# Moving the first pair of every feed-forward block to other PSUM banks, and three reorderings around it

## The reference

```python
for l in range(2):
    x = x + 0.5 * swiglu(rmsnorm(x, ffn1_norm[l]), ffn1_wg[l], ffn1_wu[l], ffn1_wd[l])   # FFN 0, FFN 2
    h = rmsnorm(x, mix_norm[l]) @ w_in[l]
    ...                                   # three attention mixers (latent, sparse, differential)
    x = x + o @ w_out[l]
    x = x + 0.5 * swiglu(rmsnorm(x, ffn2_norm[l]), ffn2_wg[l], ffn2_wu[l], ffn2_wd[l])   # FFN 1, FFN 3
x = rmsnorm(x, final_norm)
...            # a second block: dilated attention, a gated recurrence, 16 experts with chosen tokens
# swiglu(x, wg, wu, wd) = (silu(x @ wg) * (x @ wu)) @ wd, with 2816 hidden units
# rmsnorm(x, g) = x / sqrt(mean(x * x) + 1e-6) * g
```

## Time and profile before

| | value |
|---|---|
| median of 3 runs | 3041.17 us |
| lowest, highest | 3035.72, 3044.26 us |
| the profiled execution | 3043.22 us, its span 3041.4 us |
| mean granted TensorE clock | 0.978 |
| PE, DVE, ACT, POOL busy | 94%, 67%, 38%, 55% of the span |

### The profile page before, as it was taken

How to read it: one execution, slowest core, us unless ns; L and a number is a source line. 1 busy time by engine, 2 the same in 40 slices (tenths; PEclk the granted TensorE clock), 3 DMA queues, 4 the chain that set the end, 5 groups by cost and what they waited for, 6 DMA issues and landing times.

```text
span 3041.4 us, 47934 instructions
## 1 busy us (share of the span) xinstructions
PE 2859.9 (94%) x19208; PEld 2309.7 (76%) x19208; DVE 2038.9 (67%) x2752; ACT 1145.4 (38%) x2098; POOL 1682.9 (55%) x969
## 2 busy tenths in 40 slices
PE   7999999999999999999999999999998687999888
PEld 6999867668999979998666788998796675555444
DVE  8888675758888889897767589897546764112112
ACT  5333332545333353434235443434245841111111
POOL 6999744446988779784644488785443640000000
PEclk9999999999999999999999999999999888999999
DMA  4322312002232322323300032323230015999997
GB/s 154 116 93 91 132 63 105 2 2 106 96 118 91 118 84 91 117 86 118 123 23 2 29 125 85 119 89 136 83 125 1 22 42 222 407 423 423 423 423 318
DMA packets 51769, 412.44 MB, mean 136 GB/s; under 512 B 5728, under 2 KB 5984, under 8 KB 24416
## 3 DMA queue, kind: packets, MB, share of 16 engines
q1 hardware_dynamic: 51408, 408.03, 34.4%
q0 software_dynamic: 144, 1.38, 0.1%
HBM read 407.29 MB, written 2.10 MB: 135 GB/s over the span
## 4 chain that ended last, share of the span: by engine, by line
PE 71%; DVE 12%; DMA 6%; issue 5%; ACT 3%; POOL 3%; SPq 0%; DVEq 0%; ACTq 0%; POOLq 0%
PE banks L1916 7%; PE banks L1917 7%; PE banks L1918 7%; PE banks L2213 6%; PE banks L1845 6%; PE banks L1714 5%; PE banks L1933 5%; PE banks L1934 5%; PE banks L1935 5%; DMA experts<-moe_w 4%; PE banks L1793 3%; PE banks L2224 3%; PE banks L1983 2%; DMA ring<-ffn_w 2%; PE banks L2011 2%
## 5 line engine op out<-in xcount | busy, mean ns | idle before, releaser
L930 POOL TENSOR_TENSOR ring_lo<-ring,w_hi 128x1024 fp32r<-128x1024 f32 x252 | 700.3, 2792 | 154.9 <-ACT w_hi L1087 98.3
L1087 ACT ACTIVATE w_hi<-ring 128x1024 fp32r<-128x1024 f32 x256 | 270.7, 1058 | 439.9 <-PE banks L1918 430.9
L1933 PE MATMUL banks<-ffn_hidden,down_hi 128*128 128x512 f32 x704 | 276.7, 393 | 9.5 <-DVE x L2596 9.5
L1934 PE MATMUL banks<-ffn_hidden,down_hi 128*128 128x512 f32 x704 | 276.1, 392 | 0.0
L1935 PE MATMUL banks<-ffn_hidden,down_lo 128*128 128x512 f32 x704 | 275.9, 392 | 0.0
L1916 PE MATMUL banks<-t_lo,w_hi 128*128 128x256 f32 x960 | 271.9, 283 | 1.3 <-POOL ring_lo L930 1.3
L2596 DVE SCALAR_TENSOR_TENSOR x<-banks,x 128x512 f32<-128x512 f32 x352 | 230.2, 683 | 60.2 <-PE banks L1935 58.6
L1917 PE MATMUL banks<-t_hi,w_hi 128*128 128x256 f32 x960 | 269.5, 281 | 0.0
L1918 PE MATMUL banks<-t_hi,ring_lo 128*128 128x256 f32 x800 | 225.4, 282 | 0.0
L2213 PE MATMUL banks<-experts,mix 128*64 128x256 f32 x1520 | 190.4, 392 | 17.1 <-DMA experts<-moe_w 17.0
L1916 PE MATMUL banks<-upper_lo,w_hi 128*128 128x256 f32 x640 | 183.6, 287 | 19.6 <-ACT ffn_more L1170 8.7
(11 more groups left out here) (448 smaller groups left out, 8227.1 us busy)
## 6 DMA issues: line engine op xcount, KB each, us to landing
experts<-moe_w SPq DMA_DIRECT2D x47, 2048.0 KB, 18.9
ring<-ffn_w SPq DMA_DIRECT2D x43, 2048.0 KB, 7.6
experts<-moe_w SPq DMA_DIRECT2D x48, 1024.0 KB, 18.7
ring<-mix_w SPq DMA_DIRECT2D x24, 1536.0 KB, 6.4
ring<-second_w SPq DMA_DIRECT2D x16, 1536.0 KB, 6.2
ffn_more<-ffn_w SPq DMA_DIRECT2D x44, 512.0 KB, 3.8
mix<-ffn_w SPq DMA_DIRECT2D x44, 512.0 KB, 7.9
expert_table<-moe_w SPq DMA_DIRECT2D x16, 1024.0 KB, 15.6
```

The costliest lines, as they stand in the source:

```text
L930: pool.tensor_tensor(operand_lo(G, i), operand(G, i), operand_hi(G, i).bitcast(F32), ALU.subtract).then_inc(w_split, 1)
L1087: act.activation(operand_hi(G, i), operand(G, i), ACT.Copy).then_inc(w_high, 1)
L1933: mm(bank[4 + q % 4], w_hi, g[:, f, 1], start=f == 0, stop=False)
L1934: mm(bank[4 + q % 4], w_hi, g[:, f, 0], start=False, stop=False)
```

## The change

It has three parts.

1. The four tiles of pair 0 go to banks 2 to 5 instead of 0 to 3, so product 0 of pair 1 no longer waits for DVE to read banks 0 and 1; the wait for pair 0's gate and hidden units moves to product 4. Product 1 of pair 0 waits for the adds that free banks 4 and 5. Around it, lists are reordered: on ACT `high(G+1, 1)`, `high(G+1, 2)` and the two corners of product 0 come earlier; on DVE `sums(G+1, 2)` comes before the mean in FFN 0 and 2, and before the gate in FFN 1 and 3; on POOL `low(G+1, 1)` of FFN 0 comes before T3 and T2.
2. The groups of the rotation tables on POOL stand at the end of pairs 1 to 9 instead of 2 to 10, and the three `rope_reduce` of a table stand together.
3. The low parts `h_lo` of x for the mixer are made between the last adds of FFN 0 and FFN 2 instead of after them.

```diff
 POOL, pair 0
                     low(G + 1, 0)
+                    if F == 0:
+                        low(G + 1, 1)
                     t3_difference(F)
                     t2_difference(F)
-                    low(G + 1, 1, 2)
+                    if F:
+                        low(G + 1, 1)
+                    low(G + 1, 2)
                     down_low(G, 0)
 POOL, end of a pair
+                if F == 0 and j in (1, 4, 7):
+                    rope_angle(j // 3)
                 if F == 0 and j in (2, 5, 8):
-                    rope_angle(j // 3)
-                    rope_reduce(j // 3, 0)
+                    for part in range(3):
+                        rope_reduce(j // 3, part)
                 if F == 0 and j in (3, 6, 9):
-                    rope_reduce(j // 3 - 1, 1)
-                    rope_reduce(j // 3 - 1, 2)
-                if F == 0 and j in (4, 7, 10):
                     rope_ends(j // 3 - 1)
 ACT, pair 0 and pairs 1 to 10
                     high_t1(F)
+                    high(G + 1, 1)
                     act.wait_ge(mean_ready, c.next(mean_ready))
                     act.activation(rms, rms, ACT.Sqrt).then_inc(root_ready, 1)
                     load_table(ACT.Silu)
+                    high(G + 1, 2)
                     high_t3(F)
                     silu(G, 0)
-                    high(G + 1, 1)
                     high_t2(F)
-                    high(G + 1, 2)
                     down_high(G, 0)
+                    corner(G + 1, 0, 0)
+                    corner(G + 1, 0, 1)
                     high_t4(F)
                     continue
                 high(G, 3)
-                corner(G, 0, 0)
-                corner(G, 0, 1)
+                if j > 1:
+                    corner(G, 0, 0)
+                    corner(G, 0, 1)
 PE, first_product and product
-                        if i < 2 and G:
-                            pe.wait_ge((gate_scaled, hidden_ready)[a], 2 * G - 1 + i)
-                        o = two_halves(bank[a + 2 * (i % 2)])
+                        if i == 0 and G:
+                            pe.wait_ge((gate_scaled, hidden_ready)[a], 2 * G)
+                        if i == 1 and G:
+                            pe.wait_ge(down_used, KC * G - 4 + a + 1)
+                        o = two_halves(bank[2 + a + 2 * (i % 2)])
 ...
-                        if i == 0:
+                        if i == 0 and j > 1:
                             pe.wait_ge((gate_scaled, hidden_ready)[a], 2 * G - 1)
                         if i == 4:
-                            pe.wait_ge((gate_scaled, hidden_ready)[a], 2 * G)
+                            pe.wait_ge((gate_scaled, hidden_ready)[a], 2 * G if j > 1 else 2 * G - 1)
 DVE, mixer_inputs
-            x_rest(COL_MIX + 8 * l, h_hi, h_lo, *range(KC))
             x_sum(*range(1, KC))
 DVE, pair 0 (its reads of banks 0 to 3 become reads of banks 2 to 5)
                     sums(G + 1, 0, 1)
+                    if F % 2 == 0:
+                        sums(G + 1, 2)
                     dve.wait_ge(sums_ready, c.next(sums_ready))
 ...
                     step(V.reciprocal(rms, rms))
+                    if F % 2:
+                        dve.wait_ge(t_pool, 4 * F + 2)
+                        sums(G + 1, 2)
                     first_gate(G)
                     first_scaled(G)
-                    if F % 2:
-                        dve.wait_ge(t_pool, 4 * F + 2)
-                    sums(G + 1, 2)
                     first_hidden(G)
 DVE, last pair
                     add(G, q)
                     if F == 1 and q:
                         x_lows(F + 1, q - 1)
+                    if F % 2 == 0 and q:
+                        x_rest(COL_MIX + 8 * (F // 2), h_hi, h_lo, q - 1)
                 if F == 1:
                     x_lows(F + 1, KC - 1)
+                if F % 2 == 0:
+                    x_rest(COL_MIX + 8 * (F // 2), h_hi, h_lo, KC - 1)
```

More of the change, by code:

```diff
@@ L2549, in first_gate @@
                 dve.wait_ge(strassen, 2 * turn(G, 2) + 1)
-            V.tensor_tensor(GATES[0], bank[0], rms, ALU.mult).then_inc(gate_scaled, 1)
+            V.tensor_tensor(GATES[0], bank[2 if opens(G) else 0], rms, ALU.mult).then_inc(gate_scaled, 1)
         def parts(G, f, product):
@@ L2559, in first_scaled @@
                 dve.wait_ge(strassen, 2 * turn(G, 2) + 2)
-            step(V.tensor_tensor(bank[1], bank[1], rms, ALU.mult))
+            up = bank[3 if opens(G) else 1]
+            step(V.tensor_tensor(up, up, rms, ALU.mult))
         def first_hidden(G):
             dve.wait_ge(silu_ready, 2 * G + 1)
-            step(V.tensor_tensor(bank[1], bank[1], GATES[0], ALU.mult))
+            up = bank[3 if opens(G) else 1]
+            step(V.tensor_tensor(up, up, GATES[0], ALU.mult))
         def second_gate(G):
@@ L2569, in second_gate @@
             if opens(G):
-                V.tensor_tensor(GATES[1], bank[2], rms, ALU.mult).then_inc(gate_scaled, 1)
+                V.tensor_tensor(GATES[1], bank[4], rms, ALU.mult).then_inc(gate_scaled, 1)
                 return
@@ L2579, in second_hidden @@
             dve.wait_ge(strassen, pair_done(G))
+            up = bank[5 if opens(G) else 3]
             if opens(G):
-                step(V.tensor_tensor(bank[3], bank[3], rms, ALU.mult))
+                step(V.tensor_tensor(up, up, rms, ALU.mult))
             else:
@@ L2587, in second_hidden @@
             dve.wait_ge(silu_ready, 2 * G + 2)
-            step(V.tensor_tensor(bank[3], bank[3], GATES[1], ALU.mult))
-            parts(G, 1, bank[3])
+            step(V.tensor_tensor(up, up, GATES[1], ALU.mult))
+            parts(G, 1, up)
         def add(G, *list_):
@@ L2598, in ffn @@
         def ffn(F):
+            c.skip(x_high, 12)
             for j in range(FFN_PAIRS):
@@ L2608, in ffn @@
                     step(V.reciprocal(rms, rms))
+                    if F % 2:
+                        dve.wait_ge(t_pool, 4 * F + 2)
+                        sums(G + 1, 2)
                     first_gate(G)
                     first_scaled(G)
-                    if F % 2:
-                        dve.wait_ge(t_pool, 4 * F + 2)
-                    sums(G + 1, 2)
                     first_hidden(G)
-                    parts(G, 0, bank[1])
+                    parts(G, 0, bank[3])
                     make_t4(F)
@@ L2661, in ffn @@
                         x_lows(F + 1, q - 1)
+                    if F % 2 == 0 and q:
+                        x_rest(COL_MIX + 8 * (F // 2), h_hi, h_lo, q - 1)
                 if F == 1:
                     x_lows(F + 1, KC - 1)
+                if F % 2 == 0:
+                    x_rest(COL_MIX + 8 * (F // 2), h_hi, h_lo, KC - 1)
             c.one(down_used, KC * FFN_PAIRS)
             c.skip(down_ready, KC * FFN_PAIRS)
-            c.skip(x_high, 12)
         def mixed(F):
```

## The result

The changed kernel takes 3047.16 us in the median of 10 runs (3040.87 to 3055.34), the kernel before 3040.97 (3033.89 to 3047.64) beside it. The ratio is 1.0031, with a 95% interval of 1.0018 to 1.0045: slower by 0.3%, 6 us by the medians and 9 by the ratio. The forecast was 3044, with a range from 3029 to 3053. The profiled execution took 3047.59 us, span 3045.8, 4.4 us longer than the span of before.

What follows compares the result with a forecast made beforehand. PE, busy 94% of the span, was taken as the bound, so only its waits could be won. Terms of -0.4 + 4 - 1.8 + 0.9 = +2.7 us on 3041.17 gave 3043.9 us, range 3029 to 3053.

Steps and rivals of the forecast that it cites:

- The second gate: FFN 0, first pairs: DVE reaches this gate at 51.2 instead of 51.47, so product 2 starts 0.3 us sooner.
- 4 us in one piece: FFN 2, pair 1: PE idles this long ahead of product 2; the term for FFN 2 was +0.5 us.
- Part 1, size: First pairs of the four feed-forward blocks: -0.3 in FFN 0, -0.6 in FFN 1 and 3, +0.5 in FFN 2, sum -0.4 us.
- the clock cost: FFN 0, first pairs: lower PE clock costs the same as before, give or take 0.5 us.
- Tables +4 in FFN 0: FFN 0, pairs 2 to 9: POOL's regrouped tables make PE wait, +4 us, bounds -2 and +8.
- -6.8 at the mixer: First mixer: with sooner tables and nothing else changed, PE's 4.14 us wait goes and the clock is kept, -6.8 us.
- pairs 2 to 9: FFN 0: PE's gains and losses pair by pair under the moved tables, less some 1.6 us for overlap, taken as +4.
- Part 3, first mixer: x_rest(0) holds up DVE's adds, taking most of the sooner tables' gain: -1.8 us, bounds -6.8 and +1.5.
- Part 3, second mixer: Last low part of x and sums of squares end 0.9 us later: +0.9 us, bounds -0.3 and +3.
- the sum of +2.7: Whole kernel: all terms, -0.4 + 4 - 1.8 + 0.9, added to the median of 3041.17 us, giving 3043.9.
- The case at 3051: Rival: POOL becomes the bound in FFN 0 (8 us) and the lock at the mixer falls badly, +10 us; chance 0.22.

Runs made afterwards that it cites:

- e2: Part 2 alone (tables regrouped and one pair sooner) on the kernel before: ratio 0.9990 (0.9981 to 0.9999), -3.0 us.
- e1: Part 1 alone on the kernel before, tables and low parts of x as before: ratio 1.0014 (1.0005 to 1.0024), +4.3 us.
- e3: Part 3 alone on the kernel before, tables late as before: ratio 1.0011 (1.0001 to 1.0021), +3.3 us.
- e4: The changed kernel with part 3 undone, parts 1 and 2 kept: ratio to the kernel before 1.0009 (0.9999 to 1.0019).
- e9: The kernel before with the last corner's sum written to its own bank instead of SBUF: ratio 1.0024 (1.0010 to 1.0037).
- e12: The kernel before with ungrouped-as-before tables one pair sooner, 2 MB load first, last corner's sum in its bank, part 1 with corners copied sooner: ratio 1.0007.
- e8: The kernel before with tables one pair sooner in their old groups and pair 3's 2 MB load ahead of the 0.5 MB one: 0.9983, 3034.32 us.

## Why the prediction came out as it did

- *Part 1, place and order.* The gaps moved and did not close. Product 0 had no wait, and PE idled 4.55 us in one piece ahead of product 2, for L1175. The second gate stood at 51.50 where I had 51.2. I hadn't said that product 1 would wait as well (6.86 us, since product 0's corners are now behind two high parts, a silu and a down piece); product 2 starts no later for it. In FFN 2 I had 4 us in one piece ahead of product 2, and it was 2.52 and 2.68 us in two.
- *Part 1, size.* In the two traces it gives +0.3 in FFN 0, -0.4, +0.2 and -0.4 in FFN 1 to 3, so -0.3 where I had -0.4. That this agrees is luck of two executions: timed alone part 1 is +4.3 (1.5 to 7.3). This is the term that was mis-sized. Over 12 traces the first pairs are 2.0 us longer with it, for +1.3 in FFN 0 (forecast -0.3) and +1.0 in FFN 2 (forecast +0.5). I had the clock cost "the same as before, give or take 0.5" in FFN 0 and gave it no term in FFN 2, where it fell to 0.51 to 0.72 behind the gathered waits. My sum also took the landing of pair 3's weight as given, while it comes out in two ways. Whether part 1 makes the late one more frequent stays open.
- *Part 2.* Tables +4 in FFN 0 and -6.8 at the mixer make -2.8; e2 has -3.0. In FFN 0 the ledger has 3.3, and at the mixer the traces have -6.4. The pairs were guessed less well than their sum. For pairs 2 to 9 I had +1.1, +0.4, -0.5, +0.4, +0.8, +2.0, -0.6 and +2.0; by the two traces they are -1.2, +0.8, +1.7, 0.0, +0.8, +1.0, -0.7 and +0.6. That the sum came out near is in part luck. PE's waits of more than 0.4 us in these pairs grew from 3.7 to 6.1 us. The largest, 2.66 us, is in pair 4, where I had a gain of 0.5. There POOL's ends of the first table, beside DVE's sums, took 7.3 us instead of 5.45.

```profile
153.81 1.51 POOL L961 TENSOR_SCALAR table<-table 128x512 f32<-128x512 f32 x1
155.29 1.58 POOL L962 TENSOR_SCALAR table<-table 128x512 f32<-128x512 f32 x1
156.83 6.66 POOL L930 TENSOR_TENSOR even_sums<-mix,w_hi 128x1024 fp32r<-128x1024 f32 x2
```

```profile
160.19 0.39 PE L1924 MATMUL banks<-lower_lo,w_hi 128*128 128x256 f32 x1 [2.66 <-POOL even_sums L930]
```

- *Part 3, first mixer.* Forecast was h_hi(0) at 373.4, 377.1 with FFN 0's 3.7 us; it was there at 377.0. x_rest(0) fell on the bad side of the lock (2.50 us). PE entered the mixer at 384.83, 381.1 with that shift taken off, just past the 378.8 to 380.9 that I had; the lower clock that I called possible was there. The sums of squares were needed at 392.3 if that shift is taken off; forecast 390 to 393. I had -1.8 for the mixer; the ledger has -2.1.
- *Part 3, second mixer.* +0.9 forecast, +0.8 in the ledger; PE waits 0.69 us for the sum of squares there, 0.32 before.
- *The three together.* e1, e2 and e3 multiply to 1.0015, the whole is 1.0031. By e4, part 3 costs 0.22% once the tables are early, alone it costs 0.11%. Each of these ratios is uncertain by about 0.1%, so it isn't shown that the parts do more together than alone; in the traces part 3 costs much the same at the mixer, 3.5 us with late tables and 4.4 with early ones.

The mechanism at the mixers was right, and so was the place of part 1's waits; the price of the clock behind them was not, nor that of single pairs under the tables. With part 1 at e1's +4.3 instead of -0.4 the sum of +2.7 becomes +7.4, between the 6 and 9 us measured; with the 2.0 us that the traces locate it becomes +5.1. The case at 3051 came near in size, but for another cause than the one it named: POOL isn't the bound in FFN 0 (3.3 us where that case had 8).

## What to carry to other kernels

When a wait for a buffer is taken away, look at what the next instruction waits for and at which place of its engine's list its producer stands; here two copies with their operands ready stood behind silus. Look at the clock behind the new wait as well: in FFN 2 fewer idle microseconds in longer pieces made the pair longer. Interleaving work into a list pays only if its input is there at that place: a low part of x put in front of an add cost more than all it could win. And where a transfer's landing moves a stage by microseconds, read it in several traces before pricing an edit from one.

## What was unexpected of the hardware

- DVE instructions with two SBUF inputs wait for POOL to end its instruction: 2.46 us for a low part of x in the earlier trace rows, about 0.7 otherwise, and 0.42 us for the multiplication once one input stood in PSUM (e9 to e12). New is that the wait isn't limited to one instruction: with POOL's next ones queued, a DVE instruction took 6.7 to 11.9 us, until POOL had a gap or, in e2, came to an instruction of 0.2 us. There are 13 such places in seven of the 14 traces; in others, at the same place, it got in after one (1.6 to 1.9 us for the 0.43 of the multiplication). The Trainium skill (SBUF — State Buffer, "Who interferes with whom") has an exclusive lock that goes to whoever issues first; the lock agrees, the order doesn't: in e8 four POOL instructions that started after the DVE one (from 771.12 to 778.15) went ahead of it. What decides it was not found.
- The same 2 MB load took 8.25 to 10.12 us from issue to use at the same two places of the program (14 cases). With the 0.5 MB load issued behind it and not ahead of it, it took 7.4 to 7.7 us in eleven of 12 cases and 8.4 in one.
